# Twelve first-matrix panels of each squared-ReLU feed-forward, taken in pairs by seven products of quarters

## What is computed

```python
D_MODEL = 1024
D_FF = 4 * D_MODEL
def _sq_relu_mlp(h, w1, w2):
    return jnp.square(jax.nn.relu(h @ w1)) @ w2

for layer in range(DEPTH):                       # DEPTH = 2
    ...
    h = _layer_norm(DEEPNORM_ALPHA * h + mix, ln_g[layer, 0], ln_b[layer, 0])
    h = _layer_norm(DEEPNORM_ALPHA * h + _sq_relu_mlp(h, ffn_w1[layer], ffn_w2[layer]),
                    ln_g[layer, 1], ln_b[layer, 1])
```

## Time and profile before

| | us |
|---|---|
| median of 3 runs (lowest, highest) | 2817.97 (2815.57, 2818.77) |
| the profiled execution's own time | 2824.22 |
| its span | 2822.4 |
| PE busy in the span | 2716.7 (96%) |
| DVE busy | 1282.5 (45%) |
| ACT busy | 1016.7 (36%) |

### The profile page before, as it was taken

The page is one execution under the profiler, slowest core; times in us unless marked ns, Lnnn a source line. Parts: engine busy times, 40 slices in busy tenths (PEclk is TensorE's granted clock), DMA queues, the critical chain, the costliest instruction groups (busy, mean ns, idle before and its releaser), DMA issues.

```text
span 2822.4 us, 39533 instructions
## 1 busy us (share of the span) xinstructions
PE 2716.7 (96%) x16362; PEld 2368.1 (84%) x16362; DVE 1282.5 (45%) x2178; ACT 1016.7 (36%) x1630; POOL 283.9 (10%) x357
## 2 busy tenths in 40 slices
PE   8989999999999999999999999999899999999997
PEld 6877899999988888788888988888888887888886
DVE  4444563343523323464344543334666655633323
ACT  4444352223323222352233332323557543522221
POOL 0000210000300000120000310011211121200003
PEclk9999999999999999999999999999999999999998
DMA  4111233222022221323222042222321212232220
GB/s 137 46 38 50 87 98 107 90 90 90 27 71 76 75 82 60 98 82 106 97 96 97 31 155 96 83 95 71 112 88 62 92 51 91 78 109 90 97 68 31
DMA packets 66531, 232.94 MB, mean 83 GB/s; under 512 B 8880, under 2 KB 9264, under 8 KB 65968
## 3 DMA queue, kind: packets, MB, share of 16 engines
q1 hardware_dynamic: 66352, 230.41, 24.4%
HBM read 228.25 MB, written 2.10 MB: 82 GB/s over the span
## 4 chain that ended last, share of the span: by engine, by line
PE 85%; DVE 5%; ACT 4%; POOL 2%; issue 2%; DMA 1%; SPq 0%; DVEq 0%; POOLq 0%; ACTq 0%
PE ps L578 74%; PE ps L886 2%; POOL R L2628 2%; PE ps L1012 1%; PE ps L588 1%; DVE R L1890 1%; PE ps L763 1%; PE ps L724 1%; DVE HT L1884 1%; ACT HT L1236 1%; POOL S L2614 1%; PE ps L873 1%; PE ps L1109 1%; PE ps L598 1%; ACT WH L1206 1%
## 5 line engine op out<-in xcount | busy, mean ns | idle before, releaser
L578 PE MATMUL ps<-XH,WH 128*128 128x264 f32 (+2 forms) x1856 | 540.7, 334 | 15.5 <-DVE XL L2588 7.9
L578 PE MATMUL ps<-XH,LENT 128*128 128x512 f32 (+2 forms) x2096 | 532.3, 343 | 8.1 <-DVE XL L1906 7.9
L578 PE MATMUL ps<-XL,WH 128*128 128x264 f32 (+2 forms) x1856 | 526.2, 326 | 0.0
L578 PE MATMUL ps<-XH,WL 128*128 128x264 f32 (+2 forms) x1856 | 525.0, 325 | 0.0
L578 PE MATMUL ps<-HH,LENT 128*128 128x264 f32 (+2 forms) x2220 | 491.7, 319 | 1.9 <-DVE LENT L1862 1.9
L578 PEld LDWEIGHTS ps<-XH,LENT 128*128 128x128 f32 x2096 | 359.1, 190 | 60.1 <-DVE XL L1906 12.0
L1862 DVE TENSOR_TENSOR WL<-RAW,WH 128x1024 fp32r<-128x1024 f32 (+1 forms) x232 | 285.1, 1229 | 271.6 <-ACT WH L1206 271.4
L578 PEld LDWEIGHTS ps<-HH,LENT 128*128 128x128 f32 x2220 | 362.0, 190 | 31.9 <-DVE LENT L1862 2.3
L578 PEld LDWEIGHTS ps<-XH,WH 128*128 128x128 f32 x1856 | 321.8, 191 | 56.4 <-issue 9.3
L578 PEld LDWEIGHTS ps<-XH,WL 128*128 128x128 f32 x1856 | 321.3, 191 | 28.1
L578 PEld LDWEIGHTS ps<-XL,WH 128*128 128x128 f32 x1856 | 321.5, 191 | 26.6
(11 more groups left out here) (215 smaller groups left out, 2627.8 us busy)
## 6 DMA issues: line engine op xcount, KB each, us to landing
RAW<-in_wf SPq DMA_DIRECT2D x128, 512.0 KB, 3.3
RAW<-in_wr SPq DMA_DIRECT2D x48, 512.0 KB, 3.3
RAW<-in_wg SPq DMA_DIRECT2D x44, 512.0 KB, 3.2
RAW<-in_wu SPq DMA_DIRECT2D x44, 512.0 KB, 3.3
RAW<-in_wd SPq DMA_DIRECT2D x32, 512.0 KB, 3.2
RAW<-in_we SPq DMA_DIRECT2D x24, 512.0 KB, 3.3
RAW<-in_wm SPq DMA_DIRECT2D x24, 512.0 KB, 3.2
RAW<-in_wro SPq DMA_DIRECT2D x16, 512.0 KB, 3.2
```

The lines of the kernel that those rows point to most:

```text
L578: mm = e.matmul(o[:, at:at + m], wt, xt[:, k, c0 + a * m:c0 + (a + 1) * m], start=(n == 0 and j == 0), stop=(n == nk - 1 and j == 2))
```

## The change

In stages 1 to 3 of both layers the first four `wf1` panels of the stage are taken as two pairs, A (panels 0, 1) and B (panels 2, 3): six pairs in a layer, twelve in all. A pair is a product of a matrix of two by two quarters (the pair's weights: quarters of 512 x 128) and the tokens, also in two by two quarters (512 features by 264 or 256 tokens). Strassen's scheme in Winograd's form does it in seven products of quarters in place of eight: P1, P6, P5, P2, P7, P3, P4 in PE's order. Each has 4 steps of three matmuls, 12 of 264 or 256 columns, into one PSUM bank.

What it adds: sums of weight quarters, S1 to S4 of each pair, on DVE; splits of quarters and sums (512 wide, high on ACT, low on DVE) in place of splits of whole panels; sums of token quarters, T1 to T4 of each layer, on DVE, once, with their high parts by ACT and low parts by DVE, kept in buffers that also held lent slots (the ring of layer 0 loses two, that of layer 1 three); and sums of products, which go on in PSUM where they can (P2 is added onto P1, P3 onto P5's bank, P4 onto P7's), with five adds on DVE (U2, U4, C22, C12, C21). C22 reads P7's bank before P4 is added onto it, so P4 waits for C22. The relu and both squares of a pair's outputs are on ACT, DVE keeps the subtraction.

Whole panels stand between the products: in pair A `wf2` 6 and 7 of the stage before, in pair B `wf1` 4 and 5. The plan of transfers follows: `wf2` 0 to 5, `wf1` 0 and 1, `wf2` 6 and 7, `wf1` 2 to 7. The first RAW buffer of a pair comes free at S4, the second at the low split of P4. One transfer of a table for retention is moved behind the feed-forward of layer 0.

```diff
@@ weight_plan
+        out.extend(one[0])
+        for c in range(3):
+            out.extend(two[c][0:6] + one[c + 1][0:2] + two[c][6:8] + one[c + 1][2:8])
+        out.extend(two[3])
@@ the order of splits
+        UNITS.extend([(_i, 0), (_i, 1), (_i, 2), (_i + 2, None), (_i, 3), (_i, 4), (_i + 3, None), (_i, 5), (_i, 6)])
@@ when a RAW buffer is free (SP)
+    def raw_free(i):
+        if i in PAIRS:
+            return S.w_sum[i, "S4"]
+        if i in SECOND:
+            return S.part_lo[i - 1, "P4"]
+        return S.w_lo[i]
@@ PE
+        def pair(i, c0, T, freed, fill):
...
+            frees = {"P1": freed, "P6": (S.comb, i, "U2"), "P5": (S.comb, i, "C12"), "P7": (S.comb, i, "C21")}
+            behind = {"P2": S.first[i], "P3": S.comb[i, "U4"], "P4": S.comb[i, "C22"]}
+            for p in PARTS:
...
+                w.wait_ge(*S.part_lo[i, p])
...
+                    w.wait_ge(*behind[p])
+                for k in range(4):
+                    wh, wl = hi[:, k * 128:(k + 1) * 128], lo[:, k * 128:(k + 1) * 128]
+                    for n, (wt, xt) in enumerate(((wh, th), (wh, tl), (wl, th))):
+                        mm = e.matmul(o[:, 0:T2], wt, xt[:, k, :], start=(p in frees and k == 0 and n == 0),
+                                      stop=(k == 3 and n == 2), skip_group_check=True)
+                mm.then_inc(*S.part(i, p))
...
+                if p in fill:
+                    fill[p]()
@@ PE, mlp
+            for c in range(1, 4):
+                b = 32 * layer + 8 * c
+                for m in range(6):
+                    second(b - 8 + m)
+                pair(AT["wf1", b], c0, T, (S.relu, AT["wf1", b], "C11"),
+                     {"P5": lambda: second(b - 2), "P7": lambda: second(b - 1)})
+                pair(AT["wf1", b + 2], c0, T, (S.relu, AT["wf1", b + 2], "C11"),
+                     {"P5": lambda: first(b + 4), "P7": lambda: first(b + 5)})
+                first(b + 6)
+                first(b + 7)
@@ Ahead, for ACT and DVE
+        def pair(self, i):
+            for n, p in enumerate(PARTS):
+                self.units(UNIT_NO[i, n] + 1)
+                assert self.next > UNIT_NO[i, n]
+                self.upto(i + 12, 1, 1)
+                if p in SLOT_LAST:
+                    self.rel = max(self.rel, order_of((i, SLOT_LAST.index(p))))
+                yield p
@@ ACT, behind P3 (the relus of P2 and P4 likewise)
+                elif p == "P3":
+                    t = TMP[:, j % 4, T2:T]
+                    w.wait_ge(*S.comb[i, "C12"])
+                    e.activation(t, t, ACT.Relu).then_inc(*S.relu(i, "C12"))
+                    square(j, S.relu[i, "C11"], S.relu[i, "C12"])
@@ DVE, the sums of weights and the low parts
+            elif u == 4:
+                w.wait_ge(*use_done(BEFORE[i][2]))
+                e.tensor_tensor(S3, A11, A21, ALU.subtract).then_inc(*S.w_sum(i, "S3"))
+                w.wait_ge(*S.w_sum[i, "S2"])
+                e.tensor_tensor(S4, A12, PAIR_S2, ALU.subtract).then_inc(*S.w_sum(i, "S4"))
+                lower("P7", S3)
+            elif u == 5:
+                lower("P3", S4)
+            else:
+                lower("P4", A22)
@@ DVE, the sums of products
+            for p in ah.pair(i):
+                if p in dst:
+                    combine(i, p, T2, dst[p])
+                if p == "P6" and last:
+                    last()
+                if p in fill:
+                    fill[p]()
```

More of the change, by code:

```diff
@@ L77, in ffn1 @@
     def ffn1(layer):
-        for c in range(4):
-            out.extend(("wf1", 32 * layer + 8 * c + j, 8) for j in range(8))
-            out.extend(("wf2", 32 * layer + 8 * c + m, 8) for m in range(8))
+        one, two = ([[(w, 32 * layer + 8 * c + j, 8) for j in range(8)] for c in range(4)] for w in ("wf1", "wf2"))
+        out.extend(one[0])
+        for c in range(3):
+            out.extend(two[c][0:6] + one[c + 1][0:2] + two[c][6:8] + one[c + 1][2:8])
+        out.extend(two[3])
     ffn1(0)
@@ L161, in slot_plan @@
     goes = {AT["wr", 9] + 1, AT["wg1", 2] + 1, AT["wk", 1] + 1, AT["wq", 3] + 1}
-    ring, place, before, had, since = deque([("own", 0), ("own", 1), ("own", 2)]), [], [], {}, {}
+    sums = {"ln00": [("lent", 10304), ("lent", 12352)], "ln10": [("lent", 0), ("lent", 2048), ("lent", 4096)]}
+    shut = {AT["wf1", NLEAD]: "ln00", AT["wf1", 32 + NLEAD]: "ln10"}
+    opened = {AT["wf2", 27]: "ln00", AT["wf2", 59]: "ln10"}
+    ring, place, before, had, after = deque([("own", 0), ("own", 1), ("own", 2)]), [], [], {}, {}
     for i in range(NPLAN):
+        if i in shut:
+            after[shut[i]] = []
+            for s in sums[shut[i]]:
+                ring.remove(s)
+                after[shut[i]].append(had.pop(s))
+        if i in opened:
+            ring.extendleft(reversed(sums[opened[i]]))
+            for s in sums[opened[i]]:
+                had[s] = (LAST_PAIR[opened[i]], 3)
         if i in goes:
@@ L169, in slot_plan @@
             ring.extendleft(reversed(comes[i]))
[L170 to L178, removed]
+        if i in SECOND:
+            place.append(None)
+            before.append(None)
+        elif i in PAIRS:
+            four = [ring.popleft() for _ in range(4)]
+            ring.extend(four)
+            place.append(four)
+            before.append([had.get(s) for s in four])
+            for q, s in enumerate(four):
+                had[s] = (i, q)
+        else:
+            s = ring.popleft()
+            ring.append(s)
+            place.append(s)
+            before.append(had.get(s))
+            had[s] = i
+    return place, before, after
+PLACE, BEFORE, SHUT_AFTER = slot_plan()
 def final(i):
@@ L186, in lent_until, with order_of @@
 def lent_until(name, idx):
-    return max(i for i in range(AT[name, idx]) if PLACE[i][0] == "lent")
+    return max(i for i in range(AT[name, idx]) if PLACE[i] and PLACE[i][0] == "lent")
+def order_of(use):
+    return UNIT_NO[(use[0], PARTS.index(SLOT_LAST[use[1]])) if isinstance(use, tuple) else (use, None)]
 class Signal:
@@ L843, in mlp, with first, second @@
             c0, T = span(ln)
[L844 to L849, removed]
+            def first(idx):
+                drain(gemm("wf1", idx, X, x_ready(ln_in, None), c0, T, (S.relu, AT["wf1", idx], None)))
+            def second(idx, *order):
+                drain(down_block("wf2", idx, f"ff{layer}c{idx % 32 // 8}", c0, T, None, *order))
+            for j in range(NLEAD, 8):
+                first(32 * layer + j)
+            for c in range(1, 4):
[8 more added lines that the diff above has]
+                first(b + 7)
             down_norm(ln)
@@ L1465, in mlp, with first, second @@
         def mlp(layer):
-            ln = ("ln01", "ln11")[layer]
+            ln_in, ln = (("ln00", "ln01"), ("ln10", "ln11"))[layer]
             c0, T = span(ln)
[L1468 to L1474, removed]
+            for j in range(NLEAD, 8):
+                idx = 32 * layer + j
+                drain(ah.steps("wf1", idx))
+                relu2("wf1", idx, c0, T, None)
+            for c in range(1, 4):
+                b = 32 * layer + 8 * c
+                def first(j):
+                    drain(ah.steps("wf1", b + j))
+                    relu2("wf1", b + j, c0, T, None)
+                def second(m, **work):
+                    drain(ah.steps("wf2", b - 8 + m, beside=at_steps(**work)))
+                for m in range(6):
+                    second(m, s2=lambda: c == 1 and m < 4 and token_hi(ln_in, m + 1))
+                relu2_pair(b, c0, T, {"P5": lambda: second(6), "P7": lambda: second(7)})
+                relu2_pair(b + 2, c0, T, {"P5": lambda: first(4), "P7": lambda: first(5)})
+                first(6)
+                first(7)
             down_norm(ln)
@@ L2178, in mlp, with first, second @@
         def mlp(layer):
-            ln = ("ln01", "ln11")[layer]
+            ln_in, ln = (("ln00", "ln01"), ("ln10", "ln11"))[layer]
             c0, T = span(ln)
[L2181 to L2187, removed]
+            for n, j in enumerate(range(NLEAD, 8)):
+                idx = 32 * layer + j
+                sums = {5: (3, 1), 6: (2,), 7: (4,)}[j]
+                drain(ah.steps("wf1", idx, beside=at_steps(s2=lambda: [token_add(ln_in, n) for n in sums])))
+                relu2("wf1", idx, c0, T, None)
+            for n in (1, 2, 3, 4):
+                w.wait_ge(*S.t_sum[ln_in, n])
+            for c in range(1, 4):
+                b = 32 * layer + 8 * c
+                def first(j):
+                    drain(ah.steps("wf1", b + j))
+                    relu2("wf1", b + j, c0, T, None)
+                def second(m, **work):
+                    drain(ah.steps("wf2", b - 8 + m, beside=at_steps(**work)))
+                    residual("wf2", b - 8 + m, m, c0, T, None, ALPHA1 if c == 1 else None)
+                for m in range(6):
+                    second(m, s3=lambda: c == 1 and m < 4 and token_lo(ln_in, m + 1))
```

(5 more changed lines are left out.)

256 lines of the change are left out of this document (231 added, 25 removed).

## The result

The changed kernel takes 2845.34 us (median of four, 2842.41 to 2848.34) against 2817.98 before: 1.0099 times as long, 95% interval 1.0081 to 1.0116. It is slower, by 27.4 us on the medians. The profiled executions differ by 24.1 us: 2822.4 us of span before, 2846.5 now.

A forecast was written before the change was run, and what follows sets the result against it. PE bounds the kernel. Its saving of 16.3 us, against pair B's waits and clock loss, left +3.95 us a stage in layer 0 and +5.5 in layer 1: +28 us, 2846 us on the median, range 2812 to 2865.

The forecast's parts named there:

- PE saves 16.3 us: Seven products instead of two whole panels save PE 3.10 us a stage in layer 0, 2.32 in layer 1.
- 0.8 and 0.95 us before `wf1` 4: In pair B, PE waits for the split of `wf1` 4: 0.8 us in layer 0, 0.95 in layer 1.
- S4, the transfers, the splits: Pair B: S4 done at 7.9 us, `wf1` 5 landed at 11.2, P4's low part at 14.85, then splits, C22 at 25.8.
- the lower bound: Pair B, transfers landing without spacing: C22 at 24.7 us, wait 3.4 us; with no clock loss +9 us in all, 2827.
- The wait for C22, 4.5 and 5.1 us: In pair B, P4 waits for C22 on DVE: 4.5 us a stage in layer 0, 5.1 in layer 1.
- The clock, 1.75 us a pause: Behind each pause in pair B, PE's matmuls run at a lower clock, costing 1.75 us; bounds nothing and twice that.
- Later in the stage no further wait: After pair B, splits catch up during whole panels of 5.87 us each, so no further wait is found.
- The signs: Pauses of 3.4 to 5.5 us between P3 and P4 of each pair B, ended by L2300, six, granted clock below 1.00 behind.
- all is hidden: Rival: pair B's adds keep pace with PE, so the 16.3 us come whole: 2802 us; chance 0.11.
- A second wait per stage: Rival: a further wait after pair B where lent slots or RAW buffers run short; each 2 us gives 22 us, 2868; chance 0.09.

The follow-up runs named there:

- E6: Changed kernel with only pair A of each stage made by seven products, panels 2 to 7 whole again: 2811.30 us, 0.9967 times the kernel before.
- E8: Changed kernel with pair B's adds ahead of later panels' splits, P4's split before P3's and `wf1` 5's, `wf1` 4 split right behind P4 of A: 2805.81 us.
- E4: Changed kernel with ACT splitting `wf1` 4 right behind P4 of pair A, ahead of A's second panel's relu, square and copy: 2838.65 us.
- E7: Changed kernel with 24 matmuls whose result nothing reads put between P3 and P4 of each pair B, ahead of the C22 wait: 2832.64 us.
- E1: Changed kernel with no split of a later panel ahead of pair B's adds on ACT and DVE: 2827.02 us, 1.003 times the kernel before.
- E3: Changed kernel with P4's split of pair B made before P3's and `wf1` 5's, releasing the RAW buffer earlier: 2808.13 us, 0.9969 times the kernel before.
- E2: Changed kernel with no split of a later panel ahead of pair B's adds on DVE only, ACT's order kept: 2846.32 us.
- E5: Changed kernel with P4's split of pair B before P3's and `wf1` 5's, and `wf1` 4 split right behind P4 of A: 2816.24 us.

## Why the prediction was right

**The sum.** Forecast +28 us on the profiled execution; the stretches grew by 22.8, the span by 24.1. The terms add up to 5.5 us more than the stretches show: the wait for C22 was put 6.4 us too high and the saving 1.7 us too high, which pull in opposite directions, and the rest is small. That the median came out at 2845.3 against 2846 is luck: the 4.6 us by which the medians differ more than the stretches made up for it.

- *PE saves 16.3 us.* Nearly: in E6, with half the pairs, 8.4 us; in E8, with all, PE is busy for 534.1 us instead of 548.75, 14.6 less. So twelve pairs save 1.7 us less than the forecast, which took each product at half a half panel; no run shows where these lie. The Trainium skill's spacing for narrow matmuls ("TensorE: Matmul & The Clock Gate", section "Back-to-back issue gap") would have made layer 1 longer; with its pairs in E8 it is 262.8 us against 267.05, so the trace decides against it, as its rows did.
- *0.8 and 0.95 us before `wf1` 4.* Measured 4.7 us in six, 0.7 and 0.87 each; the steps as the prediction wrote them, 5.1 less 4.37 or less 3 x 1.42, give 0.73 and 0.84, closer than the values in its sum. E4 shows the cause, ACT's relu, square and copy ahead of the split.
- *S4, the transfers, the splits.* From the end of P4 of A (468.4 us in the trace): S4 forecast 7.9, measured 7.8; `wf1` 5 landed 11.2 and 11.4; P4's low part 14.85 and 15.0; C22 25.8 and 25.1. What differs is the second landing: I took 2.2 us between landings, and `wf1` 7's split came only 1.5 us after `wf1` 6's (486.76 and 488.26 on ACT; 1.3 to 1.6 in the six pairs). After that ACT and DVE set the pace: the split of `wf2` 0 waited for no transfer, and C22 came near the 24.7 of the lower bound.
- *The wait for C22, 4.5 and 5.1 us.* The mis-sized term: measured 3.3 to 3.8 in layer 0 and 3.8 to 4.3 in layer 1, 22.4 us against 28.8; the closer landings of the point above account for most of it in the pair that was followed.
- *The clock, 1.75 us a pause.* PE's busy time is 544.5 us against 534.1 for the same matmuls at a clock of 1.00 (E8): 10.3 us, 1.7 a pause. Five of the six were followed by a lower clock, so it is 2.1 for each of these; E7 gives 8.6 us in all.
- *Later in the stage no further wait.* True only behind the pause: E1 shows waits of up to 2.4 us where `wf2` 0 begins as soon as the pause is gone. I had followed the splits there, not the relus that stand between them.

**The signs.** The pauses lie where the prediction put them, between P3 and P4, ended by L2300, six in all. Two of them, 3.30 and 3.32 us, are shorter than the 3.4 that it named as the least. Behind one of the six the clock stayed at 1.00, which it had named as a sign of being wrong; behind five it fell.

**The rivals.** That all is hidden did not happen, but E8 shows that it nearly can: 2805.8 against the 2802 of that case. The point from which it decides was rightly put at C22, and so were the two reasons, C22's place behind three splits and the late start of their transfers. The experiments tell them apart: with another order and the same supply the waits for C22 go but 17.3 us of idle time remain (E1), with earlier transfers the same splits ahead of C22 leave 5.8 (E3). A second wait per stage, which I gave 0.09, was there in waiting, covered by the first; but it was for hidden features, not for slots or RAW buffers.

## What to carry to other kernels

When a change takes work from the busiest engine by giving the others more, ask for each buffer when it now comes free, and which transfer then starts late; here moving one split of half a panel two places ahead was worth 30 us in the stretches (E3). An engine that takes its instructions in order hands every delay of a transfer on to what stands behind it, so a result that the busiest engine waits for belongs ahead of preparations for later, on every engine that it passes (E1 against E2). And look for the next wait before taking one away: E2 gave nothing, and in E5 the early split took back 2.8 us of what E3 had won.

## What the runs showed that was not expected

The lower clock does not follow from the length of a pause alone. Two pauses of layer 0 in the changed kernel are nearly equal (PE's timeline, stages 2 and 3):

```profile
590.35 0.49 PE L740 MATMUL ps<-LENT,WH 128*128 128x264 f32 x2 [3.32 <-DVE TMP L2300]
...
685.63 1.66 PE L740 MATMUL ps<-LENT 128*128 128x264 f32 x6 [3.30 <-DVE TMP L2300]
```

The longer one is followed by a granted clock of 1.00 over 4.70 us, the shorter one by 0.50 over 4.40 us (fifth and sixth row of the windows after), with matmuls streaming at 1.00 ahead of both. Of the others shown, 4.40 us behind the pause of 3.80 us ran at 0.66 (third row), and 6.10 us behind one of 3.81 us in layer 1 at 0.53 (fourth row). What decides between the two was not found.
